# Changing the order of work at four places of an encoder-layer kernel: start, last attention item, slot table, last gate units

## The chip, the cores and the metric

The kernel runs on 1 core of one Trainium2 chip. The metric is the time of one execution in device microseconds. The median of 3 runs of the kernel before is 603.12 us (602.98 to 603.16).

## The reference

One encoder layer over two groups of tokens, a prompt of 512 and a sample of 256, with the same weights; 768 tokens make six tiles of 128. Model width is 1024, all in fp32.

```python
h = rmsnorm(x, norm_mix[i])
z = h @ w_in[i]                      # 1024 x 3072: q, k, v, b_g, c_g, xc
o_att  = diff_attention(q, k, v, lam, rel_bias)   # 4 heads x 2 maps
o_conv = b_g * short_conv3(c_g * xc, conv_w[i])
x = x + jnp.concatenate([o_att, o_conv], axis=-1) @ w_out[i]
h = rmsnorm(x, norm_ffn[i])
# hier_moe: top-1 of 4 groups, then top-2 of its 4 experts
for e in range(16):
    gu = t @ w_gate_up[e]            # 1024 x 512
    y = (silu(gu[:, :256]) * gu[:, 256:]) @ w_down[e]
    out = out + combine[:, e:e + 1] * y
x = x + out
e = rmsnorm(p[i] @ w_ple_proj[i], ple_norm[i])
x = x + sigmoid(x @ w_ple_gate[i]) * e
```

## The kernel before

**Precision.** Every large product is made of three fp32r matmuls: hi by hi, lo by hi and hi by lo. So each weight unit (128 x 1024 numbers, 512 KB) is split after it lands: ScalarE (ACT) writes the hi part, VectorE (DVE) subtracts it and writes the lo part. `three` (lines 509 to 511) issues the three matmuls for an output tile, `across` (539 to 541) does so for the blocks of the input projection that come out transposed.

**Stages.** First the input projection: `xT` and `w_in` are loaded, and k runs over eight slices of 128 input channels. The first block accumulates in banks 0 to 3 (512 prompt tokens each) and 4 and 5 (sample tokens, 256 columns a matmul). Ten matmuls on a zeroed fp16 tile (`warm`, line 2025) run before it. For k = 0 and 1 each bank's three matmuls stand together, and the first ones of bank 0 are written out one by one (2028, 2030, 2032). Then 24 attention items w, whose DVE steps stand in one loop over w (`scores`, `combine`, and other work placed by tables); the output projection; routing; the projection of p (`ple_proj`); and the table products. Each expert has a bin of 128 slots, and what doesn't fit goes to overflow tiles. One product of `q_hots` and `p_over` (line 2243) makes the part of the slot table for these, and `trips`, a number computed on the chip, says how many times a loop (`Fori`, from 2305) runs over overflow tiles. It runs once here. Then the expert bins t, whose outputs are put into `moe_rows` in DRAM by an indirect DMA of GpSimd (POOL), line 859.

**The end.** For each tile i of the result the two rows of each token are fetched from `moe_rows` (SyncE, SP: `pick_first` for tile 0, `pick(q)` for the others, line 754), weighted and added on DVE (`x3`, 1896), transposed by TensorE (PE, 1958), split by ACT (`x3T_hi`, 1285) and DVE (`x3T_lo`, 1907), and multiplied by the gate weights: `gate(i, q)` with q the column half. The gate weights come in eight units g = 0 to 7, (LAST + 1, g) in the code; g = 0 to 3 are used by gate(0, 0) and g = 4 to 7 by gate(0, 1), two slices k each. Units 6 and 7 lie in buffers `w_raw_more0` and `w_raw_more1`. `ple_square` (1256) sums squares of the projection of p.

**What sets the order.** Each engine executes its list in the written order and waits on semaphores. All loads except POOL's go through SP's queue, in the written order too. `pick(1)` waits for `y_st`, the landing of the last bin's put. In gate(0, 1), PE waits at every second slice for that unit's lo split (`lo_done`), and the turn of tile 1 stands before its k = 5 and its k = 7. After both, gate(1, 0) needs the splits of the turned tile.

## Time and profile before

| what | value |
|---|---|
| median of 3 runs | 603.12 us (602.98 to 603.16) |
| the profiled execution's own time | 603.42 us |
| its span in the profile | 601.6 us |
| PE busy | 593.8 us, 99% of the span |
| DVE busy | 417.6 us, 69% |
| ACT busy | 330.3 us, 55% |
| POOL busy | 68.1 us, 11% |
| DMA | 126.52 MB, mean 210 GB/s |

The profiled execution took 0.30 us more than the median, and 1.8 us of it lie outside its span. PE is busy nearly all the time, so the thing to read is where it pauses and what ends each pause. An engine's busy time says little of that; the timeline of short windows around each place that the change touches does. Matmuls overlap in the timeline: the time between two starts is what one costs on PE, not its own duration. The profile's row of granted clocks shows 9 tenths or more in every fortieth of the span.

### The profile page before, as it was taken

The numbers are of one execution on the slowest core, as the hardware profiler recorded it, in microseconds if no ns is written. First come the engines' busy times: TensorE is split into PE (matmuls) and PEld (weight loads), VectorE is DVE, ScalarE is ACT, GpSimd is POOL, SyncE is SP. The second block draws the span as 40 slices with busy tenths as digits, with TensorE's granted clock in tenths as the row PEclk, the third lists the DMA queues.
The fourth block names the chain that finished last, engine by engine and source line by source line (L and its number), as shares of the span: only waits on it lengthen the run. The fifth ranks groups of instructions, "written<-read, shape, count | busy, mean of one in ns | idle before, by whom it ended". The sixth has DMA issues, their size and how long they took to land.

```text
span 601.6 us, 8723 instructions
## 1 busy us (share of the span) xinstructions
PE 593.8 (99%) x3160; PEld 490.6 (82%) x3160; DVE 417.6 (69%) x773; ACT 330.3 (55%) x595; POOL 68.1 (11%) x109
## 2 busy tenths in 40 slices
PE   8999999999999999999999999999999999999997
PEld 6888989888887777888887887778888888878886
DVE  5426962344542666746877789899999999788863
ACT  7752200322232675656555566799999998961211
POOL 0060000000000000100100114142121220210000
PEclk9999999999999999999999999999999999999999
DMA  8916655120312412212314778989999999785611
GB/s 333 404 34 229 236 220 205 36 95 10 102 38 71 183 36 106 87 54 106 106 72 154 248 246 296 405 316 414 411 410 411 412 412 376 290 314 198 227 42 64
DMA packets 39042, 126.52 MB, mean 210 GB/s; under 512 B 6448, under 2 KB 7472, under 8 KB 38968
## 3 DMA queue, kind: packets, MB, share of 16 engines
q1 hardware_dynamic: 33224, 112.97, 50.4%
q0 software_dynamic: 4896, 12.59, 5.4%
q8 instruction: 25, 0.41, 0.3%
q10 hardware_dynamic: 880, 0.41, 0.2%
q14 instruction: 17, 0.14, 0.1%
HBM read 113.33 MB, written 23.10 MB: 227 GB/s over the span
## 4 chain that ended last, share of the span: by engine, by line
PE 93%; DMA 2%; DVE 2%; ACT 1%; issue 1%; SPq 0%; DVEq 0%; POOLq 0%; POOL 0%; ACTq 0%
PE bank L509 21%; PE bank L511 20%; PE bank L510 20%; PE bank L1958 7%; PE bank L540 6%; PE bank L541 6%; PE bank L539 5%; PE bank L1975 3%; PE bank L1994 3%; PE bank L2109 2%; PE bank L2268 1%; DMA moe_rows<-moe_y,slot_row 1%; DMA pick<-moe_rows 1%; DMA colv<-in_cols 1%; DVE w_split L1733 0%
## 5 line engine op out<-in xcount | busy, mean ns | idle before, releaser
L504 DVE TENSOR_TENSOR w_split<-w_raw,w_split 128x1024 fp32r<-128x1024 f32 x33 | 40.5, 1228 | 22.5 <-ACT w_split L499 22.3
L509 PE MATMUL bank<-w_split,moe_xT 128*128 128x512 f32 x120 | 48.4, 404 | 0.8 <-DVE w_split L1733 0.8
L1023 ACT ACTIVATE sq_tmp<-bank 128x512 f32<-128x512 f32 x12 | 7.2, 599 | 75.5 <-PE bank L511 75.5
L511 PE MATMUL bank<-w_split,moe_xT 128*128 128x512 f32 x120 | 47.0, 391 | 0.0
L510 PE MATMUL bank<-w_split,moe_xT 128*128 128x512 f32 x120 | 46.8, 390 | 0.0
L499 ACT ACTIVATE w_split<-w_raw 128x1024 fp32r<-128x1024 f32 x33 | 34.7, 1054 | 18.9 <-PE bank L541 16.6
L988 ACT ACTIVATE s<-s,mn 128x512 f32<-128x512 f32 (+1 forms) x48 | 30.9, 645 | 18.7 <-DVE mn L1441 18.7
L488 DVE TENSOR_TENSOR w_split<-w_raw_more,w_split 128x1024 fp32r<-128x1024 f32 x32 | 37.9, 1216 | 2.7 <-ACT w_split L482 2.2
L509 PE MATMUL bank<-w_split,x3T 128*128 128x512 f32 (+1 forms) x104 | 39.5, 379 | 0.2 <-DVE x3T L1907 0.2
L511 PE MATMUL bank<-w_split,x3T 128*128 128x512 f32 (+1 forms) x104 | 38.8, 373 | 0.0
L510 PE MATMUL bank<-w_split,x3T 128*128 128x512 f32 (+1 forms) x104 | 38.8, 373 | 0.0
L509 PE MATMUL bank<-w_split,h_T_prompt 128*128 128x512 f32 x96 | 38.3, 399 | 0.0
L488 DVE TENSOR_TENSOR w_split<-w_raw_room,w_split 128x1024 fp32r<-128x1024 f32 x30 | 35.7, 1217 | 3.0 <-ACT w_split L482 2.2
L511 PE MATMUL bank<-w_split,h_T_prompt 128*128 128x512 f32 x96 | 37.5, 390 | 0.0
L510 PE MATMUL bank<-w_split,h_T_prompt 128*128 128x512 f32 x96 | 37.4, 390 | 0.0
L488 DVE TENSOR_TENSOR w_split<-w_raw,w_split 128x1024 fp32r<-128x1024 f32 x30 | 35.9, 1215 | 2.0 <-issue 1.1
L539 PE MATMUL bank<-h_T_prompt,w_split 128*128 128x512 f32 x95 | 37.0, 390 | 0.0
L540 PE MATMUL bank<-h_T_prompt,w_split 128*128 128x512 f32 x95 | 37.0, 390 | 0.0
L541 PE MATMUL bank<-h_T_prompt,w_split 128*128 128x512 f32 x95 | 37.0, 389 | 0.0
L1441 DVE CUSTOM_DVE_ANT_0 s<-bank,toep 128x512 f32<-128x512 f32 (+1 forms) x48 | 27.0, 598 | 14.1 <-PE bank L1975 14.0
L482 ACT ACTIVATE w_split<-w_raw_more 128x1024 fp32r<-128x1024 f32 x32 | 33.4, 1058 | 1.5 <-PE bank L511 1.1
L482 ACT ACTIVATE w_split<-w_raw 128x1024 fp32r<-128x1024 f32 x30 | 31.6, 1061 | 1.9 <-PE bank L511 0.8
(329 smaller groups left out, 1592.1 us busy)
## 6 DMA issues: line engine op xcount, KB each, us to landing
w_raw<-in_w_moe SPq DMA_DIRECT2D x32, 512.0 KB, 5.5
w_raw_room<-in_w_moe SPq DMA_DIRECT2D x30, 512.0 KB
w_raw_more<-in_w_moe SPq DMA_DIRECT2D x30, 512.0 KB
w_raw<-in_w_in SPq DMA_DIRECT2D x23, 512.0 KB
pick<-moe_rows SPq DMA_DIRECT2D x12, 512.0 KB, 4.8
bias_rows<-bias_table SPq DMA_DIRECT2D x1, 4096.0 KB
w_raw<-in_w_out SPq DMA_DIRECT2D x8, 512.0 KB
toep<-bias_rows SPq DMA_DIRECT2D x4, 896.0 KB, 7.1
```

The lines of the kernel that those rows point to most:

```text
L482: nc.scalar.activation(W[:, WSLOT[unit], 0], src, ACT.Copy).then_inc(hi_done, 1)
L488: nc.vector.tensor_tensor(W[:, slot, 1], moe_raw(unit)[0], f(W[:, slot, 0]), ALU.subtract).then_inc(lo_done, 1)
L499: nc.scalar.activation(W[:, u % WS, 0], src, ACT.Copy).then_inc(hi_done, 1)
L504: nc.vector.tensor_tensor(W[:, u % WS, 1], raw(u)[0], f(W[:, u % WS, 0]), ALU.subtract).then_inc(lo_done, 1)
L509: nc.tensor.matmul(out, hi, whi, start=first, stop=False)
L510: nc.tensor.matmul(out, lo, whi, start=False, stop=False)
L511: return nc.tensor.matmul(out, hi, wlo, start=False, stop=last)
L539: nc.tensor.matmul(o_, w[:, 0, k % 2, tk(c)], xh, start=first and once, stop=False)
L540: nc.tensor.matmul(o_, w[:, 0, k % 2, tk(c)], xl, start=False, stop=False)
L541: ins = nc.tensor.matmul(o_, w[:, 1, k % 2, tk(c)], xh, start=False, stop=last and done)
L988: act.activation(s, s, ACT.Exp, bias=mn[:, 2 * w + m:2 * w + m + 1], scale=-1.0, accum_out=Z[:, 2 * w + m:2 * w + m + 1]).then_inc(a_e, 1)
L1958: ins = pe.transpose(out[:, q * P:(q + 1) * P], src[:, (first + q) * P:(first + q + 1) * P], ident)
```

## The change

It has four independent parts.

**Start.** SP loads the first `xT` slice in two pieces: the prompt columns (256 KB), then the first half unit of weights, then the sample columns (128 KB), with a semaphore that `gain_ffn` shares later. The hi part of that half unit is written by DVE (a copy, its first large operation) instead of ACT (line 956). There are eight warm matmuls, not ten. For k = 0 and 1 the prompt's matmuls stand by operand part: hi by hi for banks 0 to 3, then hi by lo for the four, then lo by hi, each group behind one wait. The number of matmuls is the same.

**Attention item 23.** On DVE, `scores` and `combine` of the last item now stand ahead of a convolution split (`split_conv_lo`, 1461) and of a step of routing (`top`), not around them.

**Slot table.** The product of the overflow table goes to bank 4, not bank 1, and no longer waits for the DVE splits of the loop's first tile (`lp_dxt`). PE loads `trips` earlier. In the loop, the wait for the table stands ahead of the writers of bank 4.

**End.** SP issues gate units 6 and 7 behind `pick(1)` instead of ahead of it. DVE does `x3(1)` ahead of the lo splits of units 6 and 7, and tile 0's splits between the units stand a little earlier. ACT does one sum of squares (`ple_square(3)`) after the first split of tile 0.

```diff
@@ -591,8 +591,9 @@
                               [[REL - 1, P], [P * REL, 2], [1, GW]])
                 sp.dma_start(toep[h][:], src).then_inc(toep_ld[h], 16)
 
-            sp.dma_start(xTr[0][:, 0], xT[0, :, 0]).then_inc(part_ld[0], 16)
+            sp.dma_start(xTr[0][:, 0, 0:SEQS[0]], xT[0, :, 0, 0:SEQS[0]]).then_inc(part_ld[0], 16)
             sp.dma_start(RAW[:, 0, 0], w_in[0][:, 0]).then_inc(raw_ld[0], 16)
+            sp.dma_start(xTr[0][:, 0, SEQS[0]:TOK], xT[0, :, 0, SEQS[0]:TOK]).then_inc(gain2_ld, 16)
             sp.dma_start(RAW[:, 0, 1], w_in[0][:, 1]).then_inc(xrow_ld[1], 16)
...
                 pick_first(half)
-            for g in range(4, FIN_UNITS):
+            for g in range(4, 6):
                 moe_unit((LAST + 1, g))
             x2_again(1)
             sp.wait_ge(y_st[0], 16 * 7)
             sp.wait_ge(y_st[1], 16 * 8)
             pick(1)
+            for g in range(6, FIN_UNITS):
+                moe_unit((LAST + 1, g))
             x2_again(2)
             sp.wait_ge(pe_x3, 2)
             pick(2)
...
             def x_hi_sample(k):
+                if k == 0:
+                    act.wait_ge(gain2_ld, 16)
...
             x_hi(0)
-            act.wait_ge(raw_ld[0], 16)
-            act.activation(W[:, 0, 0, 0], RAW[:, 0, 0], ACT.Copy).then_inc(a_xh, 1)
...
             y_out(LAST)
-            ple_square(3)
             for g in range(2, 4):
                 moe_hi((LAST + 1, g))
-            for half in range(2):
-                x3T_hi(0, (half,))
-                moe_hi((LAST + 1, 4 + half))
+            x3T_hi(0, (0,))
+            ple_square(3)
+            moe_hi((LAST + 1, 4))
+            x3T_hi(0, (1,))
+            moe_hi((LAST + 1, 5))
             for g in range(6, FIN_UNITS):
                 moe_hi((LAST + 1, g))
             table(ACT.Sigmoid, 5)
...
             def x_lo(k):
-                dve.wait_ge(a_xh, 2 * k + 2 if k else 1)
+                dve.wait_ge(a_xh, 2 * k + 1)
                 dve.scalar_tensor_tensor(out=hTp[:, 1, k], in0=xTr[k // 2][:, k % 2, 0:SEQS[0]],
...
 
             def x_lo_sample(k):
-                dve.wait_ge(a_xh, 2 * k + 3)
+                dve.wait_ge(a_xh, 2 * k + 2)
                 dve.scalar_tensor_tensor(out=hTs[:, 1, k], in0=xTr[k // 2][:, k % 2, SEQS[0]:TOK],
...
 
+            dve.wait_ge(raw_ld[0], 16)
+            dve.tensor_copy(W[:, 0, 0, 0], RAW[:, 0, 0]).then_inc(d_xl, 1)
             dve.wait_ge(gain_ld, 16)
             x_lo(0)
-            dve.wait_ge(a_xh, 2)
+            dve.wait_ge(d_xl, 1)
             dve.tensor_tensor(W[:, 0, 1, 0], RAW[:, 0, 0], f(W[:, 0, 0, 0]),
                               ALU.subtract).then_inc(d_xl, 1)
...
@@ -1638,11 +1644,14 @@
             link(dve.memset(r_C[:, 0], 0.0))
             link(dve.memset(slots[:], float(SKIP)))
             for w in range(1, NI + 1):
+                if w == NI - 1:
+                    scores(w)
+                    combine(w)
                 if w - 1 in O_AT:
                     mix_lo(O_AT[w - 1])
                 if w in ROUTE_AT:
                     logits(ROUTE_AT[w])
-                if 2 <= w < NI:
+                if 2 <= w < NI - 1:
                     scores(w)
                 if w in LATE_UNITS:
                     split_lo(LATE_UNITS[w])
@@ -1662,7 +1671,7 @@
                     tile_hots(ROUTE_AT[w] - 1)
                 if w in TOP_AT:
                     top(*TOP_AT[w])
-                if w < NI:
+                if w < NI - 1:
                     combine(w)
             logits(TILES - 3)
             x2_sum(TILES - 2, 1)
...
             dve.wait_ge(pe_tab, 2)
-            link(dve.tensor_tensor(val_f[:, over], slots[:, E:], bank[1][:, 0:COLS - E - 1], ALU.add))
+            link(dve.tensor_tensor(val_f[:, over], slots[:, E:], bank[4][:, 0:COLS - E - 1], ALU.add))
...
@@ -1916,14 +1925,17 @@
 
             x3_first(0)
             x3_first(1)
-            for g in range(3):
+            for g in range(2):
                 moe_lo((LAST + 1, g))
             x3T_lo(0, (0,))
+            moe_lo((LAST + 1, 2))
+            x3T_lo(0, (1,))
             moe_lo((LAST + 1, 3))
-            x3T_lo(0, (1,))
-            for g in range(4, FIN_UNITS):
+            for g in range(4, 6):
                 moe_lo((LAST + 1, g))
             x3(1)
+            for g in range(6, FIN_UNITS):
+                moe_lo((LAST + 1, g))
             x3T_lo(1)
             x3(2)
...
             pe.wait_ge(dch, 2)
-            for _ in range(10):
+            for _ in range(8):
                 pe.matmul(bank[7][:], warm[:, 0:P], warm[:, P:5 * P], start=True, stop=True)
             w = W[:, 0]
-            pe.wait_ge(a_xh, 2)
-            pe.matmul(bank[0][:], w[:, 0, 0, tk(0)], hTp[:, 0, 0], start=True, stop=False)
+            pe.wait_ge(a_xh, 1)
             pe.wait_ge(d_xl, 1)
-            pe.matmul(bank[0][:], w[:, 0, 0, tk(0)], hTp[:, 1, 0], start=False, stop=False)
+            for c in range(PROMPT_TILES):
+                pe.matmul(bank[c][:], w[:, 0, 0, tk(c)], hTp[:, 0, 0], start=True, stop=False)
             pe.wait_ge(d_xl, 2)
-            pe.matmul(bank[0][:], w[:, 1, 0, tk(0)], hTp[:, 0, 0], start=False, stop=False)
-            for u, i, ks in ([(0, i, (k,)) for k in range(2) for i in range(TILES)]
+            for c in range(PROMPT_TILES):
+                pe.matmul(bank[c][:], w[:, 0, 0, tk(c)], hTp[:, 1, 0], start=False, stop=False)
+            pe.wait_ge(d_xl, 3)
+            for c in range(PROMPT_TILES):
+                pe.matmul(bank[c][:], w[:, 1, 0, tk(c)], hTp[:, 0, 0], start=False, stop=False)
+            for i in range(PROMPT_TILES, TILES):
...
+                across(bank[i], i, 0, w, True, False)
+            pe.wait_ge(a_xh, 3)
+            pe.wait_ge(hi_done, 1)
+            for c in range(PROMPT_TILES):
+                pe.matmul(bank[c][:], w[:, 0, 1, tk(c)], hTp[:, 0, 1], start=False, stop=False)
+            pe.wait_ge(d_xl, 5)
+            for c in range(PROMPT_TILES):
+                pe.matmul(bank[c][:], w[:, 0, 1, tk(c)], hTp[:, 1, 1], start=False, stop=False)
+            pe.wait_ge(lo_done, 1)
+            for c in range(PROMPT_TILES):
+                pe.matmul(bank[c][:], w[:, 1, 1, tk(c)], hTp[:, 0, 1], start=False, stop=False)
+            for u, i, ks in ([(0, i, (1,)) for i in range(PROMPT_TILES, TILES)]
                              + [(u, i, (2 * u, 2 * u + 1)) for u in range(1, 4) for i in range(TILES)]):
...
                     for k in ks:
-                        if i == k == 0:
-                            continue
                         if i == 0:
-                            pe.wait_ge(d_xl, 2 * k + 2)
-                            if k > 0:
-                                pe.wait_ge(lo_done, u + 1)
+                            pe.wait_ge(d_xl, 2 * k + 3)
+                            pe.wait_ge(lo_done, u + 1)
                         elif i == PROMPT_TILES:
-                            pe.wait_ge(d_xl, 2 * k + 3)
+                            pe.wait_ge(d_xl, 2 * k + 4)
                         ins = across(bank[i], i, k, W[:, u], k == 0, k == KD - 1)
                     if u == 3:
...
 
+            pe.wait_ge(d_route, 1)
+            n = pe.value_load(trips[0:1, 0:1], min_val=1, max_val=OVER_TILES + 1)
...
-            pe.wait_ge(lp_dxt, 2)
             for c in range(6):
-                ins = pe.matmul(bank[1][:, 0:COLS - E - 1], q_hots[:, c],
+                ins = pe.matmul(bank[4][:, 0:COLS - E - 1], q_hots[:, c],
                                 p_over[:, c].rearrange("p l e -> p (l e)"), start=(c == 0), stop=(c == 5))
             ins.then_inc(pe_tab, 1)
 
-
-            pe.wait_ge(d_route, 1)
-            n = pe.value_load(trips[0:1, 0:1], min_val=1, max_val=OVER_TILES + 1)
 
...
+                pe.wait_ge(d_tab, 4)
                 for half in range(2):
                     pe.wait_ge(lp_aat, i * 2 + (half + 1))
                     pe.wait_ge(lp_ld[4 + half], i * 16 + 16)
                     raw_down(half, act32, lp_y)
-                pe.wait_ge(d_tab, 4)
                 pe.wait_ge(lp_xg, i * 16 + 32)
                 loop_turn()
```

PE at the start of the program: bank0 to bank3 are the prompt's output tiles, `act_x_hi` and `dve_x_lo` the semaphores of the first splits. Before:

```order
L2025 MATMUL bank7<-warm_ops_212 128x512 x9
L2028 MATMUL bank0<-h_T_prompt_51,w_split_49 128x512 [waits act_x_hi]
L2030 MATMUL bank0<-h_T_prompt_51,w_split_49 128x512 [waits dve_x_lo]
L2032 MATMUL bank0<-h_T_prompt_51,w_split_49 128x512 [waits dve_x_lo]
L539 MATMUL bank1<-h_T_prompt_51,w_split_49 128x512
L540 MATMUL bank1<-h_T_prompt_51,w_split_49 128x512
L541 MATMUL bank1<-h_T_prompt_51,w_split_49 128x512
L539 MATMUL bank2<-h_T_prompt_51,w_split_49 128x512
L540 MATMUL bank2<-h_T_prompt_51,w_split_49 128x512
L541 MATMUL bank2<-h_T_prompt_51,w_split_49 128x512
L539 MATMUL bank3<-h_T_prompt_51,w_split_49 128x512
```

After:

```order
L2037 MATMUL bank7<-warm_ops_212 128x512 x7
L2042 MATMUL bank0<-h_T_prompt_51,w_split_49 128x512 [waits dve_x_lo,act_x_hi]
L2042 MATMUL bank1<-h_T_prompt_51,w_split_49 128x512
L2042 MATMUL bank2<-h_T_prompt_51,w_split_49 128x512
L2042 MATMUL bank3<-h_T_prompt_51,w_split_49 128x512
L2045 MATMUL bank0<-h_T_prompt_51,w_split_49 128x512 [waits dve_x_lo]
L2045 MATMUL bank1<-h_T_prompt_51,w_split_49 128x512
L2045 MATMUL bank2<-h_T_prompt_51,w_split_49 128x512
L2045 MATMUL bank3<-h_T_prompt_51,w_split_49 128x512
L2048 MATMUL bank0<-h_T_prompt_51,w_split_49 128x512 [waits dve_x_lo]
L2048 MATMUL bank1<-h_T_prompt_51,w_split_49 128x512
L2048 MATMUL bank2<-h_T_prompt_51,w_split_49 128x512
L2048 MATMUL bank3<-h_T_prompt_51,w_split_49 128x512
```

The weights' hi part now comes through `dve_x_lo`; four matmuls stand between one wait and the next.

PE between the projection of p and the loop over overflow tiles: the row with bank1 (before) or bank4 (after) and `pair_over` is the table product, TENSOR_LOAD the load of `trips`. Before:

```order
L1958 MATMUL bank6<-cst_209,moe_x_first_159 128x128 [waits moe_x_loaded1,act_ple]
L1958 MATMUL bank6<-cst_209,moe_x_first_159 128x128 x3
L1958 MATMUL bank7<-cst_209,moe_x_first_159 128x128 x4
L2243 MATMUL bank1<-pair_over_200,over_rank_hot_129 128x80 [waits loop_dve_xT_lo,dve_one_hots]
L2243 MATMUL bank1<-pair_over_200,over_rank_hot_129 128x80 x5
L2249 TENSOR_LOAD trips_259 [waits dve_routed]
L2249 ISA x2
L2305 UNCONDITIONAL_BRANCH [waits act_ple]
L2305 ISA
L2308 ISA [waits loop_dve_xT_lo]
L509 MATMUL bank0<-w_split_49,moe_xT0_165 128x512 [waits loop_w_lo]
```

After, from the last matmuls ahead of the load on:

```order
L511 MATMUL bank6<-w_split_49,p_T_132 128x512
L2260 TENSOR_LOAD trips_259 [waits dve_routed]
L2260 ISA x2
...
L1970 MATMUL bank7<-cst_209,moe_x_first_159 128x128 x4
L2270 MATMUL bank4<-pair_over_200,over_rank_hot_129 128x80 [waits dve_one_hots]
L2270 MATMUL bank4<-pair_over_200,over_rank_hot_129 128x80 x5
L2329 UNCONDITIONAL_BRANCH [waits act_ple]
L2329 ISA
L2332 ISA [waits loop_dve_xT_lo]
L509 MATMUL bank0<-w_split_49,moe_xT0_165 128x512 [waits loop_w_lo]
```

The load is moved ahead of a step of the projection of p, and the product lost its wait on the tile's lo split.

SP at the end of the program: w_raw_more0 and w_raw_more1 are gate units 6 and 7, rows to pick0_0 and pick1_0 are `pick(1)`. Before:

```order
L674 DMA w_raw_50<-in_w_gate 128x1024 [waits w_lo_done] x2
L674 DMA w_raw_more0_142<-in_w_gate 128x1024 [waits w_lo_done]
L674 DMA w_raw_more1_143<-in_w_gate 128x1024 [waits w_lo_done]
L749 DMA x2_1_80<-x2_rows 128x1024 [waits w_lo_done]
L754 DMA pick0_0_176<-moe_rows 128x1024 [waits y_stored1,y_stored0]
L754 DMA pick1_0_178<-moe_rows 128x1024
L749 DMA x2_2_81<-x2_rows 128x1024 [waits w_lo_done]
L754 DMA pick0_1_177<-moe_rows 128x1024 [waits pe_x3T]
```

After:

```order
L675 DMA w_raw_50<-in_w_gate 128x1024 [waits w_lo_done] x2
L750 DMA x2_1_80<-x2_rows 128x1024 [waits w_lo_done]
L755 DMA pick0_0_176<-moe_rows 128x1024 [waits y_stored1,y_stored0]
L755 DMA pick1_0_178<-moe_rows 128x1024
L675 DMA w_raw_more0_142<-in_w_gate 128x1024 [waits w_lo_done]
L675 DMA w_raw_more1_143<-in_w_gate 128x1024 [waits w_lo_done]
L750 DMA x2_2_81<-x2_rows 128x1024 [waits w_lo_done]
L755 DMA pick0_1_177<-moe_rows 128x1024 [waits pe_x3T]
```

Units 6 and 7 moved behind the picks that wait for the last put.

## Rows read from the trace of the kernel before

**Rows 1.** The page's busy times: engine, us, share of the span, count.
```profile
PE 593.8 (99%) x3160; PEld 490.6 (82%) x3160; DVE 417.6 (69%) x773; ACT 330.3 (55%) x595; POOL 68.1 (11%) x109
```

**Rows 2.** Timeline at the start: start us, us, engine line op out<-in xcount [idle before <-releaser].
```profile
1.40 4.45 PE L2025 MATMUL bank<-warm_ops 128*128 128x512 f16 x10 [1.40 <-DVE warm_ops L1328]
...
4.23 0.72 ACT L935 ACTIVATE h_T_prompt<-x_T,colv 128x512 fp32r<-128x512 f32 x1 [1.53 <-DMA colv<-in_cols]
...
4.86 0.61 ACT L956 ACTIVATE w_split<-w_raw 128x512 fp32r<-128x512 f32 x1
...
5.53 0.63 PE L2028 MATMUL bank<-h_T_prompt,w_split 128*128 128x512 f32 x1
5.77 0.68 DVE L1345 TENSOR_TENSOR w_split<-w_raw,w_split 128x512 fp32r<-128x512 f32 x1
...
10.34 0.40 PE L539 MATMUL bank<-h_T_prompt,w_split 128*128 128x512 f32 x1
...
12.18 1.23 DVE L504 TENSOR_TENSOR w_split<-w_raw,w_split 128x1024 fp32r<-128x1024 f32 x1 [0.16 <-ACT w_split L499]
...
14.52 0.40 PE L539 MATMUL bank<-h_T_prompt,w_split 128*128 128x512 f32 x1
```

**Rows 3.** Timeline at the last attention item, same columns.
```profile
328.31 0.48 DVE L1456 SCALAR_TENSOR_TENSOR s<-s,ratio,s 128x256 f32<-128x256 f32 x1
328.38 0.40 PE L511 MATMUL bank<-w_split,mix_att 128*128 128x512 f32 x1
...
328.90 0.41 PE L1958 MATMUL bank<-cst,s 128*128 128x128 f32 x2
```

**Rows 4.** Timeline from the table product to the loop's turn of act.
```profile
366.50 1.28 DVE L1773 TENSOR_TENSOR moe_xT<-bank,moe_xT 128x512 fp32r<-128x512 f32 x2
...
367.93 0.38 PE L2243 MATMUL bank<-pair_over,over_rank_hot 128*128 128x80 f16 x6 [0.29 <-DVE moe_xT L1773]
...
369.12 0.49 PE L509 MATMUL bank<-w_split,moe_xT 128*128 128x512 f32 x1 [0.81 <-DVE w_split L1733]
```

**Rows 5.** The same timeline, some microseconds later.
```profile
373.08 1.21 DVE L1800 TENSOR_TENSOR w_split<-w_raw,w_split 128x1024 fp32r<-128x1024 f32 x1
...
375.30 0.42 DVE L1778 TENSOR_TENSOR moe_act<-bank,moe_silu 128x256 f32<-128x256 f32 x1 [1.01 <-issue]
...
375.78 0.44 PE L1958 MATMUL bank<-cst,moe_act 128*128 128x128 f32 x2 [0.26 <-issue]
```

**Rows 6.** Who reads trips: line engine op, durations in ns, first and last start.
```profile
L2249 PEldq TENSOR_LOAD <-trips x1: 488/488/488, 368.0 to 368.0; - x1
```

**Rows 7.** The chain that ended last, near the end: start us, us, what.
```profile
523.31 6.55 DMA moe_rows<-moe_y,slot_row
```

**Rows 8.** DMA queues from 521 to 523.6 us: packets, MB, share of 16 engines.
```profile
q1 hardware_dynamic: 283, 1.03, 101.7%
```

**Rows 9.** The puts of line 859: time from issue to landing.
```profile
DMA to landing us min/median/max: 3.4/7.1/9.3
```

**Rows 10.** Timeline at the end, columns as in rows 2.
```profile
528.06 2.00 ACT L482 ACTIVATE w_split<-w_raw_more 128x1024 fp32r<-128x1024 f32 x2
...
530.68 2.35 DVE L488 TENSOR_TENSOR w_split<-w_raw_more,w_split 128x1024 fp32r<-128x1024 f32 x2
...
534.85 2.99 DVE L1896 SCALAR_TENSOR_TENSOR x<-pick,wgt,x 128x512 f32<-128x512 f32 x4 [1.82 <-DMA pick<-moe_rows]
...
535.10 0.39 PE L509 MATMUL bank<-w_split,x3T 128*128 128x512 f32 x1
...
536.86 0.48 PE L509 MATMUL bank<-w_split,x3T 128*128 128x512 f32 x1
...
537.20 0.60 ACT L1285 ACTIVATE x3T<-bank 128x512 fp32r<-128x512 f32 x1 [3.40 <-PE bank L1958]
...
537.83 0.69 DVE L1907 TENSOR_TENSOR x3T<-bank,x3T 128x512 fp32r<-128x512 f32 x1
...
539.46 0.40 PE L509 MATMUL bank<-w_split,x3T 128*128 128x512 f32 x1
```

5 lines of the change are left out of this document (3 added, 2 removed).

## Prediction

> **What bounds the kernel now.** I read the page's busy times first: PE is busy 593.8 of 601.6 us [rows 1], so a microsecond off another engine is worth nothing unless PE paused for it. Then I read the timeline around each of the four places, for the starts of PE's matmuls and what stands in brackets behind them. Four pauses are touched. At the start PE has its first real matmul at 5.53 and begins the second weight unit at 14.52 [rows 2]. At the last attention item it turns the combined scores at 328.90, one slot after the matmul of 328.38 should have ended [rows 3]. Around the table it pauses 0.29 us before the product and 0.81 us before the loop [rows 4], and again before the turn of act at 375.78 [rows 5]. At the end the chain of waits leaves PE for a put of 6.55 us [rows 7], the picks, and the sums on DVE at 534.85 [rows 10]; PE is held there until the turn, and its k = 5 starts at 536.86 though it is issued one turn after 535.10. The changed kernel does the same number of matmuls, so the forecast is the sum of what happens to these pauses.
>
> **Prices used throughout.** From 10.34 to 14.52 PE does all of k = 1, twelve matmuls of 512 columns and twelve of 256 [rows 2]: 4.18 us. Shared out by columns and with a little more for the short ones, that is near 0.228 us for 512 columns and 0.12 us for 256. The ten warm matmuls take 4.45 us with the last one's tail, some 0.43 us each from start to start [rows 2]. A column in 0.84 ns is TensorE at 1.2 GHz, a column in 0.45 ns is near 2.4 GHz: the warm ones run at the lower of its two levels, the later ones at the higher. From DVE's end to PE's start it takes 0.15 us (366.50 + 1.28 = 367.78 to 367.93, [rows 4]).
>
> **Start: a gain of 0.62.** Before, k = 0 and k = 1 take 14.52 - 5.53 = 8.99 us for 2 x 4.18 = 8.36 us of work, so stalls and the slow level cost 0.63. After, PE's first group needs ACT's x_hi, which ends at 4.23 + 0.72 = 4.95 [rows 2], and the hi part of the weights from DVE. That half unit now travels behind 128 KB less. It had landed at 4.86 at the latest, when ACT began to read it, but ACT was only then free. At the 397 GB/s that the queue moves in a full stretch (1.03 MB in 2.6 us, [rows 8]) 128 KB are 0.33 us, so it lands by 4.53. The copy on DVE has no row before: it is bounded by 0 below and by the two-source subtraction of the same tile, 0.68 [rows 2], above; at the upper end it ends at 5.21, at the lower ACT's 4.95 decides. I take 5.0 to 5.2, so PE starts at 5.15, 0.38 earlier. The lo parts then come from DVE while four matmuls of the first group run, and the sample slice, which lands later than before, isn't needed until twelve matmuls later. I let two matmuls still run at the lower level, 0.2 us each over the price: before, stalls and slow matmuls together cost only 0.63, so it can't have been more than three. End of k = 1: 5.15 + 8.36 + 0.4 = 13.91 instead of 14.52, a gain of 0.61, taken as 0.62 with rounding. What could hold it: the lo split of the next unit ends at 12.18 + 1.23 = 13.41 [rows 2], plus 0.15; it has 0.35 us of room, and is what is late next. One more DMA is issued by SP ahead of it, which the full queues hide. Bounds: a gain of 0.96 (the split's end decides), a loss of 1.1 if the higher level comes later.
>
> The subtraction of 128 x 512 takes 0.68 us [rows 2]. The Trainium skill, VectorE: DVE Perf Modes, section "The perf-mode tier table (the rule you actually need)", says that a one-source fp32 copy within SBUF runs at about twice the rate of a two-source operation; by it the copy would be an estimated 0.34 us, and PE's start would go by ACT's 4.95 alone, within the 5.15 above. No row of before shows such a copy.
>
> **Attention item 23: a gain of 0.29.** DVE's combine ends at 328.31 + 0.48 = 328.79 and PE turns it at 328.90; the matmul before started at 328.38, so PE was free at 328.61 [rows 3]. After, combine stands ahead of a convolution split and a routing step, with nothing between it and the exponentials that DVE had sat waiting beyond; the 0.29 us goes whole. What moves behind is a split and a routing step whose readers come later. Bounds: 0 (if a later DVE step holds PE instead) to 0.29.
>
> **Slot table: a gain of 1.0.** Before, the product waits for the lo split of the loop's tile, ending 367.78, and starts at 367.93; then comes the load of `trips`, 0.49 us [rows 6], and the loop begins at 369.12 [rows 4]. That row names a DVE split as the releaser, but the first matmul waits for the first split only, done long before: the pause of 0.81 is the load with what follows it. After, the product needs no tile and runs in the time in which PE waited, and the load is paid four microseconds earlier, where DVE's chain to 367.78 runs on; there it may hold PE for 0 to 0.81, hidden unless the tile's splits are held too. I take 0.26 for it, all hidden. The loop's first matmul then starts at 367.78 + 0.15 plus its branch, about 368.05, 1.07 earlier. But the gain must also pass the turn of act: DVE's split ends at 373.08 + 1.21 = 374.29, and the product of act (0.42, then 0.06 to the turn: 375.30 + 0.42 to 375.78) can't begin before [rows 5]. So the turn comes at 374.29 + 0.48 = 374.77 instead of 375.78: 1.0. Bounds: 0 (the load costs where it goes what it cost where it was) to 1.15. The moved wait for the table in the loop is met by then, at no cost: the table's sums stand on DVE ahead of that split.
>
> **End: a loss of 1.57.** Units 6 and 7 (1 MB) leave the queue ahead of the last put, and x3(1) comes ahead of their splits. Two things follow.
>
> First, the put. It takes 6.55 us [rows 7], a put with the queues nearly empty 3.4 [rows 9]. While it waits, the queue of SP's loads takes the whole of the engines, 101.7% [rows 8]. With 1 MB less, 2.6 us of that queue are gone. Best case, landing at 523.31 + 3.4 = 526.7; the last put shares with another, so I take 527.4 (529.86 before). DVE's sums then start at S = 527.4 + 4.99 (before: 529.86 to 534.85) = 532.4.
>
> Second, the units. The lo split of unit 6 now stands behind x3(1): S + 2.99 + 1.17 (half of 2.35, [rows 10]) + 0.15 gives PE its k = 4 of unit 6 at X = 536.7, where before it came at 535.10 without a wait. DVE is no longer ahead. The turn of tile 1 then follows three matmuls later with no wait of its own (0.68 + 0.41 us), so k = 5 starts at 537.8 instead of 536.86: a loss of 0.93. The pause that goes comes back larger under another name. Break-even is a put that lands at 526.5.
>
> Then ACT. Unit 7 lands two and a half microseconds behind the picks (1 MB at 397 GB/s), S + 2.5; its hi split takes 1.0 (half of 2.00), and the activation table and two sums of squares behind it 537.20 - 3.40 - (528.06 + 2.00) = 3.74 us [rows 10]. So ACT turns to tile 1's hi split at S + 7.3 = 539.7, where PE's turn would allow S + 5.8. Before, the lo split of that half ended at 537.83 + 0.69 = 538.52 and gate(1, 0) began at 539.46 [rows 10], so 0.94 of it is room: 1.5 - 0.94, near 0.64 with the handoffs, is a second pause. Sum 0.93 + 0.64 = 1.57. For a landing of 526.7 it is 0.87, of 529.86 it is 4.0, and 0 if the picks come early enough for all.
>
> **Sum.** -0.62 - 0.29 - 1.0 + 1.57 = -0.34 us. The profiled execution took 603.42, so 603.08 for its like; it lies 0.30 above the median, and the measurement is of medians: 603.12 - 0.34 = **602.8**.
>
> **Rivals.**
> - **A, the end works as meant** (chance 0.17): the put lands by 526.5 and unit 6 is split before PE asks. For it: 3.4 us on an idle queue; against it: two puts together, and 2.99 us of sums ahead of the split. The end costs 0 to -0.5, total near 600.8.
> - **B, the put doesn't come earlier** (0.16), the slower side: its landing stays at 529.86, X = 539.2, the end costs 4.0 and the kernel takes 603.12 - 1.91 + 4.0 = 605.2. It decides from a landing later than 529.0. Against it: the full queue of SP [rows 8] in which the put got nothing. For it: the time of a put isn't proportional to what is queued (3.4 to 9.3, [rows 9]). The Trainium skill, DMA: Bandwidth & Descriptors, section "Queues, rings and completion order", says that each engine goes round its queues packet by packet; by that rule the put would have had its share from the first, and taking loads away would help it little. The trace disagrees for these 2.6 us, and so I give it no more.
> - **D, the table part gives nothing** (0.07): the load holds the turns of the loop's tile, and the total is 603.8.
>
> **Chances.** My forecast has 0.52, spread over 601.9 to 604.0, with its lower tail (0.12) below 601.9. A measurement of this kernel can tell 0.2%, 1.2 us, from no change. Faster than 601.9: A and that tail, 0.29. Slower than 604.3: B, most of C and the upper tail, 0.24. Between: 0.47. The range, 600.8 to 605.3, leaves out the better half of A and the worse half of B.
>
> **What would show it.** At the start, PE's first real matmul near 5.15 and the second unit at 13.9. At item 23, no pause before the turn. At the table, the product ahead of 367.8 and the loop's first matmul 1.0 earlier. At the end, the put's landing (4.99 us before the sums), PE waiting on a DVE split of w_raw_more in gate(0, 1), and a wait of gate(1, 0) on the splits of tile 1. I am wrong if that split is not waited for, or if the put's piece stays at 6.5 us.

## The result: slower by 0.33%, and the runs spread

The changed kernel takes 604.74 us, the median of 13 runs (602.58 to 607.26); the kernel before takes 602.87 in its 13 (602.19 to 603.61). The ratio is 1.0033, with a 95% interval of 1.0019 to 1.0048: slower by some 1.9 us. I had forecast 602.8, a little faster, with a range of 600.8 to 605.3. The time lies in the range, the sign is wrong.

Two things stand beside the median. The runs of the kernel before lie within 1.4 us of each other, those of the changed one spread over 4.7. And the changed kernel's runs show a mean granted clock between 0.993 and 1.0 (the average over the whole run, as a share of full speed): seven of them are below 0.999, from 604.21 us upward; the six at 1.0 take 602.58 to 604.74. The six at 1.0 average 603.8 us, the four at 0.996 or 0.997 605.2, the three at 0.993 606.6. So the time goes with the clock, and the runs at full clock are still 0.9 us above before. One execution in the experiments below, of the kernel with the table part alone, took 658.22 us at a clock of 0.849 and is left out of its numbers. The profiled execution is the fastest of the 13, 602.58 us with a span of 600.8, which is 0.8 under the span of before (601.6). So the trace below shows what the change does in its best case, and the experiments have to show the rest. The page of that execution, busy times:

```profile
PE 592.8 (99%) x3158; PEld 490.2 (82%) x3158; DVE 418.0 (70%) x774; ACT 329.7 (55%) x594; POOL 67.9 (11%) x109
```

The timeline at the start, with the columns start us, us, engine line op out<-in xcount [idle before <-releaser] (the rows answer to [rows 2]):

```profile
1.40 3.60 PE L2037 MATMUL bank<-warm_ops 128*128 128x512 f16 x8 [1.40 <-DVE warm_ops L1332]
...
3.82 0.72 ACT L938 ACTIVATE h_T_prompt<-x_T,colv 128x512 fp32r<-128x512 f32 x1 [1.12 <-DMA colv<-in_cols]
...
4.41 0.43 DVE L1347 CAST w_split<-w_raw 128x512 fp32r<-128x512 f32 x1 [3.07 <-DMA w_raw<-in_w_in]
...
4.98 1.18 PE L2042 MATMUL bank<-h_T_prompt,w_split 128*128 128x512 f32 x4
...
12.30 1.22 DVE L504 TENSOR_TENSOR w_split<-w_raw,w_split 128x1024 fp32r<-128x1024 f32 x1 [0.16 <-ACT w_split L499]
...
13.68 0.47 PE L539 MATMUL bank<-h_T_prompt,w_split 128*128 128x512 f32 x1
```

PE's first real matmul starts at 4.98 instead of 5.53 and the second weight unit at 13.68 instead of 14.52, 0.84 us earlier. The copy on DVE takes 0.43 us. At 13.68 the unit's lo split (12.30 + 1.22) has just ended, as the first part of the prediction had it next in line.

At the last attention item and at the table (answering to [rows 3 to 5]):

```profile
327.82 0.38 PE L1970 MATMUL bank<-cst,s 128*128 128x128 f32 x2
```

```profile
365.38 1.29 DVE L1782 TENSOR_TENSOR moe_xT<-bank,moe_xT 128x512 fp32r<-128x512 f32 x2
...
366.56 0.38 PE L2270 MATMUL bank<-pair_over,over_rank_hot 128*128 128x80 f16 x6
...
366.82 0.49 PE L509 MATMUL bank<-w_split,moe_xT 128*128 128x512 f32 x1
...
373.10 0.42 DVE L1787 TENSOR_TENSOR moe_act<-bank,moe_silu 128x256 f32<-128x256 f32 x1
...
373.57 0.44 PE L1970 MATMUL bank<-cst,moe_act 128*128 128x128 f32 x2 [0.30 <-DVE moe_act L1787]
```

The turn of the scores has no bracket and no pause any more. The table product runs ahead of the end of the tile's lo split (365.38 + 1.29 = 366.67) and the loop starts right behind it, at 366.82. The turn of act is at 373.57, 2.21 before its old place, while the turn of the scores, upstream of the table part, is 1.08 earlier (328.90 to 327.82): the table part gives 1.1 here.

At the end, the chain of waits has a put of 2.92 us where [rows 7] had 6.55, and then another DMA, the load of unit 7:

```profile
520.61 2.92 DMA moe_rows<-moe_y,slot_row
...
524.92 7.53 DMA w_raw_more<-in_w_gate
```

The timeline there (answering to [rows 10]):

```profile
523.60 0.80 SPq L755 DMA_DIRECT2D pick<-moe_rows  x2
...
529.07 2.98 DVE L1905 SCALAR_TENSOR_TENSOR x<-pick,wgt,x 128x512 f32<-128x512 f32 x4
...
531.18 1.06 ACT L482 ACTIVATE w_split<-w_raw_more 128x1024 fp32r<-128x1024 f32 x1 [5.21 <-DMA w_raw_more<-in_w_gate]
...
532.28 2.50 DVE L488 TENSOR_TENSOR w_split<-w_raw_more,w_split 128x1024 fp32r<-128x1024 f32 x2 [0.23 <-ACT w_split L482]
...
533.56 0.50 PE L509 MATMUL bank<-w_split,x3T 128*128 128x512 f32 x1 [0.99 <-DVE w_split L488]
...
537.17 1.06 ACT L1288 ACTIVATE x3T<-bank 128x512 fp32r<-128x512 f32 x2
...
538.52 0.50 PE L509 MATMUL bank<-w_split,x3T 128*128 128x512 f32 x1 [1.03 <-DVE x3T L1916]
```

The put lands at 523.5, the picks are issued at 523.60, and the sums run from 529.07 to 532.05. Unit 6's lo split starts at 532.28, right behind ACT's hi split of that unit (531.18 + 1.06), which had waited for the unit's load. So in this execution the landing of unit 6 ends last, 0.2 us behind the sums; my forecast had only the sums in that place. PE waits 1.15 us over its slot for unit 6 (matmul of 533.56) and 1.2 us for the splits of tile 1 (matmul of 538.52). These are the two pauses that I had forecast. The old one, 0.66 us over its slot at the turn of tile 1, is gone, so the first costs 0.49 net where I had 0.93, and the second costs 1.2 where I had 0.64.

One thing gains that the forecast had no term for: the pause ahead of gate(0, 0). From the start of the last eight matmuls ahead of it to its first one it took 1.28 us, and now takes 0.81. Before:

```profile
525.53 1.06 PE L2359 MATMUL bank<-late_rank_hotT,moe_y 128*128 128x128 f32 x8
...
526.81 0.50 PE L509 MATMUL bank<-w_split,x3T 128*128 128x512 f32 x1 [0.23 <-DVE x3T L1907]
```

After:

```profile
523.34 1.06 PE L2383 MATMUL bank<-late_rank_hotT,moe_y 128*128 128x128 f32 x8
...
524.15 0.48 PE L509 MATMUL bank<-w_split,x3T 128*128 128x512 f32 x1
```

### The profile page after: what moved, and what is told of

The parts are those of the page before. It is cut to its first block, busy times and chain, and to the rows that moved or that the text cites. A ratio compares the mean times of both kernels' runs of the same rounds, so it can differ in the third digit from the quotient of the medians.

```text
span 600.8 us, 8720 instructions
## 1 busy us (share of the span) xinstructions
PE 592.8 (99%) x3158; PEld 490.2 (82%) x3158; DVE 418.0 (70%) x774; ACT 329.7 (55%) x594; POOL 67.9 (11%) x109
## 4 chain that ended last, share of the span: by engine, by line
PE 93%; DVE 3%; DMA 2%; ACT 1%; issue 1%; SPq 0%; DVEq 0%; POOLq 0%; ACTq 0%
PE bank L509 20%; PE bank L511 19%; PE bank L510 19%; PE bank L1970 7%; PE bank L539 5%; PE bank L541 5%; PE bank L540 5%; PE bank L1987 3%; PE bank L2006 3%; PE bank L2135 2%; DMA w_raw_more<-in_w_gate 1%; PE bank L2292 1%; DVE w_split L1742 1%; PE bank L2037 1%; DMA moe_rows<-moe_y,slot_row 0%
## 5 line engine op out<-in xcount | busy, mean ns | idle before, releaser
L510 PE MATMUL bank<-w_split,x3T 128*128 128x512 f32 (+1 forms) x104 | 38.8, 373 | 0.0
L539 PE MATMUL bank<-h_T_prompt,w_split 128*128 128x512 f32 x88 | 34.4, 391 | 0.1
L540 PE MATMUL bank<-h_T_prompt,w_split 128*128 128x512 f32 x88 | 34.3, 390 | 0.0
L541 PE MATMUL bank<-h_T_prompt,w_split 128*128 128x512 f32 x88 | 34.2, 389 | 0.0
```

The lines of the kernel that those rows point to most:

```text
L510: nc.tensor.matmul(out, lo, whi, start=False, stop=False)
L539: nc.tensor.matmul(o_, w[:, 0, k % 2, tk(c)], xh, start=first and once, stop=False)
L540: nc.tensor.matmul(o_, w[:, 0, k % 2, tk(c)], xl, start=False, stop=False)
L541: ins = nc.tensor.matmul(o_, w[:, 1, k % 2, tk(c)], xh, start=False, stop=last and done)
```

## Experiments

Theory 1 was that the granted clock falls or rises late at the start (rival C of the prediction); theory 2 that the end is to blame. Each kernel below was timed beside the kernel before, on the same chip as it; two kernels of different groups can have run on different chips, so compare what each has over before.

**The start alone, on the kernel before.** The start's edits as in the diff above, nothing else.

> The kernel before with the start part alone (split first load, copy on DVE, eight warm matmuls, k = 0 and 1 by operand part). Theory 1, the clock at the start: PE is granted its higher level later in many runs, so the median is some 2 us above before (604.5 to 605.5), the runs spread over 3 to 4 us and many show a granted clock of 0.993 to 0.997. Theory 2, the end is to blame: this kernel is 0.6 to 0.9 us faster than before, its runs within 1 us of each other, all at 1.0.

Measured: 602.45 us (601.32 to 603.48, 11 runs) beside 603.16 (602.42 to 603.68); ratio 0.9992 (0.9983 to 1.0001). All runs at 0.999 or 1.0. Theory 1 falls: the start is no loss, and in the medians a gain of 0.7 us, with no change just inside the interval. Its runs spread over 2.2 us, where theory 2 had expected 1.

**All but the start.** The changed kernel with the start of before.

> The changed kernel with the start of before; the other three parts stay. Theory 1: the spread is gone and the granted clock is 1.0 in all runs; the time is that of before plus -0.3 (item 23), -1.1 (table) and +1.3 (end), so 602.8, within 0.5 us of before. Theory 2: the spread stays (602 to 607) and the median is 2 to 3 us above before.

Measured: 605.14 us (603.38 to 606.4, 11 runs) beside 603.16, ratio 1.0029 (1.0017 to 1.004). The spread stays, and five runs show 0.996 or 0.997, all above 605.1. Theory 2, at the lower edge of its 2 to 3 us.

**The end alone, on the kernel before.** The three hunks of SP, ACT and DVE at the end.

> The kernel before with the end part alone. Theory 1: 1.3 us above before (604.2), runs close together, clock 1.0. Theory 2: 2 to 4 us above before, runs spread over 3 us or more, some with a clock below 1.0.

Measured: 606.86 us (605.2 to 607.31, 5 runs) beside 603.16, ratio 1.0061 (1.0047 to 1.0075). The end alone costs 3.7 us. Of its runs the profiled one is the fastest, 605.2; its timeline:

```profile
526.09 0.80 SPq L754 DMA_DIRECT2D pick<-moe_rows  x2
...
532.60 2.99 DVE L1899 SCALAR_TENSOR_TENSOR x<-pick,wgt,x 128x512 f32<-128x512 f32 x4 [0.95 <-DMA pick<-moe_rows]
...
536.78 0.50 PE L509 MATMUL bank<-w_split,x3T 128*128 128x512 f32 x1 [1.72 <-DVE w_split L488]
...
541.15 0.50 PE L509 MATMUL bank<-w_split,x3T 128*128 128x512 f32 x1 [0.42 <-DVE x3T L1910]
```

No code upstream differs from before here (PE is some 0.3 us later all the same, as at the turn of act, 376.05 against 375.78), so the forecast's own terms can be read off. Sums at 532.60 (forecast 532.4), PE on unit 6 at 536.78 (536.7), then a pause ahead of gate(1, 0). The span is 603.4, 1.8 over before, where I had 1.57. The mechanism and its size stand for this execution. The two runs at full clock, 605.20 and 605.64, are 2.0 and 2.5 over before. But the median is 3.7 over before, and the three runs at 606.86 and above all show a clock of 0.997.

**Ten warm matmuls in the changed kernel.**

```diff
-            for _ in range(8):
+            for _ in range(10):
                 pe.matmul(bank[7][:], warm[:, 0:P], warm[:, P:5 * P], start=True, stop=True)
```

> The changed kernel with ten warm matmuls instead of eight, which closes the idle stretch of PE before its first real matmul. Theory 1, in the form that the idle stretch or the shorter warm-up is the cause: clock 1.0 in all runs, 602.3 to 602.8. If it is the time at which PE does its real work and not the warm-up, the spread of the changed kernel stays, with 604 to 605. Theory 2 expects no difference to the changed kernel, 604.7.

Measured: 604.19 us (602.41 to 606.56, 11 runs) beside 603.16, ratio 1.0022 (1.0008 to 1.0037); the spread and the runs at 0.996 and 0.997 stay. The idle stretch before the first real matmul isn't what makes the low clock.

**All but the end.** The changed kernel with the end of before.

> The changed kernel with the end of before; start, item 23 and table stay. Theory: the end alone is to blame, so this keeps the three gains, 0.7 + 0.3 + 1.1, and is 1.5 to 2.1 us below before (601.0 to 601.7 on a chip where before takes 603.2), runs within 1.5 us, clock 0.999 to 1.0. Rival: the last put lands when it did, whatever stands upstream, and the gain ends there: within 0.7 us of before.

Measured: 602.05 us (600.6 to 603.86, 11 runs) beside 602.88 (602.54 to 603.65), ratio 0.9987 (0.9978 to 0.9996), clock 0.999 or 1.0 throughout. The sign turns: the other three parts gain. But only 0.8 us in the medians, against the 1.5 to 2.1 that I expected, where their gains in the traces sum to 2.2 and this kernel's own profiled run (601.02, span 599.2) has 2.4. The profiled run of before (603.42) lies 0.5 above the median here, and this kernel's lies 1.0 below its own, so 1.6 of the 2.4 is not in the medians.

**The sums of squares ahead of units 6 and 7**, in the end-only kernel:

```diff
-            for g in range(6, FIN_UNITS):
-                moe_hi((LAST + 1, g))
             table(ACT.Sigmoid, 5)
             ple_square(4)
             ple_square(5)
+            for g in range(6, FIN_UNITS):
+                moe_hi((LAST + 1, g))
```

> The kernel before with the end part alone, and on ACT the activation table and the two sums of squares moved ahead of the hi splits of units 6 and 7, where ACT sits idle for 5.3 us. Theory: the second pause of PE, 0.8 us between the matmuls at 540.33 and 541.15 of the end-only kernel (0.6 over its slot), goes; 0.6 us less than the end-only kernel, 606.2, and the first pause stays at 1.9 over its slot. Rival: the second pause has another cause (the sums of tile 1), and stays.

Measured: 605.27 us (603.77 to 607.98, 6 runs) beside 602.88, ratio 1.0046 (1.0028 to 1.0064); half of the runs at 0.997. Timeline of the profiled one:

```profile
533.71 1.06 ACT L482 ACTIVATE w_split<-w_raw_more 128x1024 fp32r<-128x1024 f32 x1 [1.62 <-DMA w_raw_more<-in_w_gate]
...
536.08 0.50 PE L509 MATMUL bank<-w_split,x3T 128*128 128x512 f32 x1 [1.15 <-DVE w_split L488]
...
537.59 0.60 ACT L1287 ACTIVATE x3T<-bank 128x512 fp32r<-128x512 f32 x1 [1.52 <-PE bank L1964]
```

ACT now splits tile 1 as soon as PE has turned it, and no PE matmul behind 536.08 has a wait in its row. So the second pause was ACT's table and squares, as forecast. The first stays, 1.15 us here. Three runs still show 0.997 although the second pause is gone from the traced one, so a low clock doesn't seem to need it; no trace was taken of those three. Six runs are too few to size it in the medians.

**Idle PE filled**, in the end-only kernel: eight matmuls without use, into a bank that nobody reads any more, just ahead of the wait for unit 6.

```diff
+                    if i == 0 and half == 1 and k == 4:
+                        for _ in range(8):
+                            pe.matmul(bank[4][:], x3T[0][0][:, 0], W[:, WSLOT[LAST + 1, 4], 0, 0, 0:N],
+                                      start=True, stop=True)
                     if i == 0 and k % 2 == 0:
                         pe.wait_ge(lo_done, MOE0 + AT[LAST + 1, g] + 1)
```

> The kernel before with the end part alone, and eight matmuls of 512 columns without use on PE just ahead of the wait on unit 6, so that PE works 1.82 us of the 1.9 to 3 us in which it waited. Theory (the pause lets TensorE's clock fall to the lower of its levels, which costs 1.5 to 2 us in the runs that show 0.997): the clock is at 0.999 or 1.0 in all runs and the time is 604.8 to 605.6, below the end-only kernel's 606.9 though PE does more. Rival (the slow runs come from a later landing, not from the clock): 606.9 or more, some runs at 0.997.

Measured: 605.03 us (604.75 to 606.49, 5 runs) beside 602.88, ratio 1.0038 (1.0025 to 1.0051). All runs at 0.999 or 1.0. PE does 1.8 us more work and the kernel costs 2.15 over before instead of 3.7, as much as the end-only kernel's two runs at full clock (2.0 and 2.5). What the useless matmuls save is not waiting, it is the clock. One run, 606.49 at 1.0, is slow without a low clock.

**DVE's order of before, SP's new one**, in the end-only kernel: units 6 and 7 split ahead of `x3(1)`.

```diff
-            x3(1)
             for g in range(6, FIN_UNITS):
                 moe_lo((LAST + 1, g))
+            x3(1)
```

> The kernel before with the end part, but on DVE the splits of units 6 and 7 ahead of the sums of tile 1, as before the change. Theory (either one holds PE: the sums of 2.99 us or the landing of the units 1.2 us after the picks): the first pause shrinks by some 1.7 us for unit 6, but the sums of tile 1 start behind the split of unit 7, near 536.2, end at 539.2, and PE waits there for some 3 us before its first turn: 2 us slower than the end-only kernel, 608 to 609. Rival (only the order on DVE was at fault): 603.5 to 604.

Measured: 608.28 us (605.82 to 609.0, 6 runs) beside 602.88, ratio 1.0083 (1.0068 to 1.0097); five of six runs at 0.994 to 0.997. The pause at unit 6 is 1.11 us, not the 0.2 that I expected: unit 6 lands late (its load is issued at 526.64, ACT begins on it at 533.50). A second one of 1.76 comes at the turn of tile 1. So the cost moves to the turn and grows: with the new load order, either order on DVE holds PE. This run's trace caught the fall of the clock. The timeline, then a table by stretch (us, busy of PE, PEld, DVE, ACT and POOL, PEclk, DMA share, GB/s):

```profile
535.88 0.50 PE L509 MATMUL bank<-w_split,x3T 128*128 128x512 f32 x1 [1.11 <-DVE w_split L488]
...
538.62 1.12 PE L1964 MATMUL bank<-cst,x 128*128 128x128 f32 x4 [1.76 <-DVE x L1899]
...
539.96 0.63 PE L510 MATMUL bank<-w_split,x3T 128*128 128x512 f32 x1
...
540.38 0.63 PE L511 MATMUL bank<-w_split,x3T 128*128 128x512 f32 x1
...
540.81 0.63 PE L509 MATMUL bank<-w_split,x3T 128*128 128x512 f32 x1
...
542.59 0.39 PE L510 MATMUL bank<-w_split,x3T 128*128 128x512 f32 x1
```

```profile
530.00:534.30 4.30, 4.30 (x21) 3.56 (x20) 1.35 (x2) 0.80 (x1) 0.00 (x0) 1.00 1.00 393
536.50:538.60 2.10, 0.36 (x2) 0.00 (x0) 2.06 (x4) 2.06 (x5) 0.00 (x0) 0.93 1.03 421
538.60:541.60 3.00, 2.98 (x9) 2.57 (x10) 2.07 (x3) 1.58 (x3) 1.81 (x2) 0.50 0.31 101
541.90:544.00 2.10, 2.10 (x13) 1.78 (x12) 0.81 (x2) 1.44 (x3) 0.00 (x0) 1.00 0.98 361
```

After two pauses with three matmuls between them, the 512-column matmuls start 0.43 us apart (540.38 to 540.81), as the warm ones do at the start, and the granted clock of the stretch 538.6 to 541.6 is 0.50, that is 1.2 GHz. While PE worked ahead of the pauses, and from 541.9 on, it is 1.00, or 2.4 GHz; in the second pause itself it begins to fall, 0.93. Three microseconds at half speed are an estimated 1.5 us lost.

**The table part alone.**

> The kernel before with the table part alone: product into bank 4 without the wait, trips loaded earlier, the loop's wait for the table moved. Theory: the 1.0 to 1.1 us gained by the turn of act stays to the end, 1.0 us below before, all runs at 0.999 or 1.0. Rival: part of it is lost again at the first picks or the last put, whose landings don't move with PE: 0.3 to 0.6 below before, and a wider spread than before's 1.1 us.

Measured: 602.35 us (601.54 to 603.5, 11 runs) beside 602.9 (602.17 to 603.61), ratio 0.9991 (0.9982 to 1.0). That is 0.55 us in the medians, as the rival had it, but a gain of 1.0 us is still inside the interval. In its trace the way from the turn of the scores (329.33) to the turn of act (375.11) takes 45.78 us, where before it took 46.88 (328.90 to 375.78): the 1.1 is there in the trace.

**A small part of the end kept.** The changed kernel with SP's order of before and `x3(1)` behind all splits; what stays of the end is that tile 0 is split earlier between the units and one sum of squares later.

```diff
-            for g in range(4, 6):
+            for g in range(4, FIN_UNITS):
                 moe_unit((LAST + 1, g))
...
             pick(1)
-            for g in range(6, FIN_UNITS):
-                moe_unit((LAST + 1, g))
...
-            x3(1)
             for g in range(6, FIN_UNITS):
                 moe_lo((LAST + 1, g))
+            x3(1)
```

> The changed kernel with SP's order of before (units 6 and 7 ahead of the picks) and the sums of tile 1 behind all splits, as before; of the end part only the reordering of tile 0's splits and of one sum of squares stays. Theory: the pause of 0.96 between starts at the gate's beginning (523.79 in the kernel without the end part) is mostly gone, but the turn of tile 1 still waits for the put and the picks, so what is won at the gate's beginning is lost again there: within 0.3 us of the kernel without the end part, that is 0.8 to 1.2 below before. Rival: the gain arrives, 0.4 us or more below that kernel.

Measured: 601.48 us (600.71 to 602.42, 10 runs) beside 602.9, ratio 0.9979 (0.9969 to 0.9988). This version beats both kernels and lies 1.4 us under before, more than the 0.8 to 1.2 that I expected. Its rows at the end:

```profile
527.20 0.80 SPq L755 DMA_DIRECT2D pick<-moe_rows  x2
...
532.12 3.03 DVE L1903 SCALAR_TENSOR_TENSOR x<-pick,wgt,x 128x512 f32<-128x512 f32 x4 [0.57 <-DMA pick<-moe_rows]
...
533.75 0.66 PE L1968 MATMUL bank<-cst,x 128*128 128x128 f32 x4 [0.39 <-DVE x L1903]
```

One pause is left, at the turn of tile 1, behind the picks; there is none for the units. The span is 598.9, 0.3 under that of the kernel without the end part.

**SP's order of before, DVE's new one**, in the changed kernel: the first two pieces of the last diff without its third.

> The changed kernel with SP's order of before alone; DVE still sums tile 1 ahead of the splits of units 6 and 7. Theory (the sums ahead of the splits hold PE whatever the loads do, and the put lands later behind 1 MB of loads): the sums start near 533, unit 6 is split 4.2 us later, PE waits 3.5 to 4 us there, the clock falls in most runs: 2.5 to 4.5 us above before. Rival (the late landing of the units was what held PE): no longer than before, 0.5 to 1 us below it.

Measured: 606.4 us (605.39 to 607.85, 5 runs) beside 602.9, ratio 1.0066 (1.0053 to 1.0079); all five runs at 0.994 to 0.997. The units are there early and PE waits all the same: it is `x3(1)` ahead of their splits that holds it. Timeline and table by stretch:

```profile
526.88 0.80 SPq L755 DMA_DIRECT2D pick<-moe_rows  x2
...
531.90 2.99 DVE L1903 SCALAR_TENSOR_TENSOR x<-pick,wgt,x 128x512 f32<-128x512 f32 x4 [2.72 <-DMA pick<-moe_rows]
...
534.81 2.35 DVE L488 TENSOR_TENSOR w_split<-w_raw_more,w_split 128x1024 fp32r<-128x1024 f32 x2
...
536.08 0.50 PE L509 MATMUL bank<-w_split,x3T 128*128 128x512 f32 x1 [3.48 <-DVE w_split L488]
...
537.95 0.63 PE L511 MATMUL bank<-w_split,x3T 128*128 128x512 f32 x1
...
538.38 0.63 PE L509 MATMUL bank<-w_split,x3T 128*128 128x512 f32 x1
```

```profile
532.30:536.00 3.70, 0.30 (x2) 0.00 (x0) 3.63 (x6) 0.00 (x0) 1.59 (x1) 1.00 1.03 422
536.00:537.50 1.50, 1.42 (x8) 1.24 (x9) 1.16 (x2) 0.00 (x0) 0.00 (x0) 1.00 1.00 407
537.50:541.00 3.50, 3.50 (x12) 2.77 (x12) 0.69 (x1) 0.85 (x2) 0.00 (x0) 0.51 0.71 287
```

PE stands for 3.48 us until 536.08, starts again at full speed for 1.5 us, and only then runs 3.5 us at a granted clock of 0.51: an estimated 1.7 us lost. The Trainium skill, TensorE: Matmul & The Clock Gate, section "HAM oscillation — how this bites in real kernels", tells of a kernel whose waits for data inside the kernel let the clock drop again, so that the next stretch of work starts slow. The two tables agree that it drops (0.50 and 0.51), but the second has the next stretch start at 1.00 for 1.5 us, and there the measurement decides.

**Both repairs in the changed kernel**: the sums of squares early and the idle PE filled.

> The changed kernel with both repairs of its end: ACT's table and sums of squares ahead of the hi splits of units 6 and 7, and eight matmuls without use on PE ahead of its wait on unit 6. Theory (the pause of PE and the fall of TensorE's clock after it make the slow half of the changed kernel's runs, 0.993 to 0.997): every run at 0.999 or 1.0, none above 604.5, median 602.6 to 603.6. Rival (the slow half comes from landings that vary with the start or the table part): median 604.2 or more, runs up to 606 and 607 remain, with or without a clock below 0.999.

Measured: 603.33 us (602.63 to 604.81, 11 runs) beside 603.1 (602.53 to 603.57), ratio 1.0006 (0.9997 to 1.0015). Every run at 0.999 or 1.0; one, 604.81, lies above the 604.5 that I had as the limit. The timeline:

```profile
524.15 0.80 SPq L755 DMA_DIRECT2D pick<-moe_rows  x2
...
530.93 2.99 DVE L1905 SCALAR_TENSOR_TENSOR x<-pick,wgt,x 128x512 f32<-128x512 f32 x4 [1.64 <-DMA pick<-moe_rows]
...
532.54 1.98 PE L2402 MATMUL bank<-w_split,x3T 128*128 128x512 f32 x8
...
535.11 0.50 PE L509 MATMUL bank<-w_split,x3T 128*128 128x512 f32 x1 [0.60 <-DVE w_split L488]
```

With two edits that shorten no chain ahead of unit 6, the loss of 0.33% is down to what can't be told from none, and the runs at 606 and 607 are gone. The first pause is still there behind the useless matmuls. This kernel doesn't tell the two edits apart. An estimate from the other runs: the changed kernel's runs at full clock have a median 1.0 over before, this one has 0.2, so 0.7 of the 1.6 us won would be the second pause and 0.9 the clock.

## Why the prediction failed, by its own steps

**What bounds the kernel; the four places:** right. All of the change happened where the pauses were read.

**Start, a gain of 0.62:** right in kind, 0.84 in the trace and 0.7 in the medians of the kernel with the start alone. PE started at 4.98, not 5.15, and what held the second unit was the lo split, which I had as the bound on the gain. The copy took 0.43 us, between the bounds 0 and 0.68. By the Trainium skill, VectorE: DVE Perf Modes, section "The perf-mode tier table (the rule you actually need)", I had estimated 0.34, half of the 0.68. That halved too much: the subtraction takes 0.68 us for 512 columns and 1.22 for 1024, so about 0.14 of it doesn't grow with the columns, and 0.14 plus half of the rest gives an estimated 0.41. Rival C, the clock at the start, did not happen: in the trace the first groups of four start at 4.98, 6.00 and 6.91, that is 0.23 to 0.26 us a matmul. Its 3.5 us of delay stand in no run.

**Item 23, a gain of 0.29:** the pause of 0.29 is gone in the trace. It was not timed alone.

**Table, a gain of 1.0:** 1.1 in the trace at the turn of act. The medians of the kernel with this part alone give 0.55 us, which the interval doesn't tell from 1.0 us.

**End, a loss of 1.57:** the mechanism and the size held where the clock did, in part by luck. In the end-only kernel the sums came at 532.60 against 532.4, unit 6 at 536.78 against 536.7, the span grew by 1.8. Two terms on the way were each wrong and cancelled: the put took 2.9 us, not the 4.1 of my 527.4 landing (it starts at 523.11 there and the picks are issued at 526.09), and from the picks' issue to the sums it took 6.5 us in place of 4.9, now that 1 MB of units stands in the queue right behind the picks. With the units ahead it is 5.0 (526.88 to 531.90). Two more terms were missing and of opposite sign: the landing of unit 6, which holds its split in the changed kernel's trace and in that of the kernel with the splits first, and the 0.47 us gained ahead of gate(0, 0).

**The sum: here it fails, in two terms.** It put the time at 0.3 us under before, and the median came 1.9 over.

**First, it has no term for the clock after the pauses.** I read PE's clock only at the start, in a rival with 0.08, and priced the two pauses at the end by their length. In about half of the changed kernel's runs the granted clock is low, and where a trace of a relative caught it (one kernel with pauses of 1.11 and 1.76 us, one with a single pause of 3.48) it falls to half for 3.0 and 3.5 us, an estimated 1.5 to 1.7 us lost. A mean of 0.997 over 604 us is an estimated 1.8 us of full clock missing, one such fall, and 0.993 is 4.2, more than two. The changed kernel's averages, 603.8, 605.2 and 606.6, step up by 1.4 each. The filled kernel takes it away: 3.7 us over before becomes 2.15, the difference 1.55, and none of the 16 runs with useless matmuls has a low clock. The old kernel has a pause at this place too, but 0.66 us over its slot, and no run under 0.999. No trace was taken of the changed kernel itself in a run with a low clock, so that its fall stands at the same place is inferred from its relatives (the two tables above, and the filled kernels). This term makes about 1 us of the changed kernel's average; its six runs at full clock are still 0.9 over before, and would have missed the sign, too.

**Second, the gains of 1.91 don't reach the median.** Without the end part the medians give 0.8, and 1.4 in the version with tile 0's splits moved. The two intervals overlap, and the profiled runs of the two differ by only 0.3, so the difference of 0.6 is not shown to be real. The traces have the whole gain (spans of 599.2 and 598.9 against 601.6), the medians of 10 or 11 runs lack more than 1 us of it, and the cause stays open. The kernels with some of these three parts spread over 1.7 to 3.3 us where before spreads over 1.0 to 1.4, at a full clock. A landing that varies would do that: the end-only kernel, the repaired one and the changed one differ by 1.3 us from the picks' issue to the sums, and the last put starts 2.2 us ahead of PE's last eight matmuls before gate(0, 0) in the trace of before, 2.7 with the start alone and 1.8 without the end part. It wasn't tested.

**The rivals:** A (the end works) is out: PE waits in every trace. B (the put stays) is out: 2.9 us. D (the table part gives nothing) is out in the traces: 1.1. The loss that came was of the size I had given B, for another reason. That the time lies in the stated range is luck: the range reaches that far up for rival B, a put that stays late, and not for a lower clock at the end.

## What to carry over

Price a new pause of the matmul engine twice: by its length, and by what the clock may do after it; here pauses of 1 to 2 us cost another 1.5 in half of the runs. And don't take a gain read off one trace for a gain of the median: that trace can lie a microsecond to one side. When a loss shows more in the median than in the profiled run, read the granted clock of all runs before the trace. When work is moved ahead of splits on an in-order engine, check who is next in line on PE: here, with the new load order, either order of the sums and the two splits held PE.
